# A hybrid decoder step on eight cores: feature-major residual, packed weights, six token tiles, grouped attention and three merged mixer streams

## What is computed

```python
xp = xp + 0.5 * half_ffn(xp, *ffn1)                       # silu(h @ w_gate) * (h @ w_up) @ w_down
qa, ka, va, hq, hf, hi, mq, zg = split_in(rmsnorm(xp, g_mix[l]) @ w_in[l])
for g, (win, dil) in enumerate(((128, 1), (512, 4), (2048, 16))):
    o, s = dilated_group_prompt(qa[:, :, g], ka[:, :, g], va[:, :, g], win, dil)   # 128-query blocks, own and previous block
att = combine_groups(outs, lses)                          # weighted by the softmax denominators
q, k, v, logf = hgrn2_gates(hq, hf, hi, lb)               # f = lb + (1 - lb) * sigmoid(z_f), q = sigmoid(z_q)
o_hg, S = hgrn2_prompt(q, k, v, logf)                     # S_t = diag(f_t) S_{t-1} + k_t v_t^T, chunks of 64
mk, mv = mem_kv(mem_prompt, g_mem[l], w_mem_k[l], w_mem_v[l])
o_mem = mem_attend(mem_heads(mq), mk, mv)                 # 256 memory tokens
xp = xp + merge_branches(att, head_rmsnorm(o_hg, g_hg_out[l]), o_mem, zg, *bw)     # 3 sigmoid gates, then w_out
xp = xp + 0.5 * half_ffn(xp, *ffn2)
```

## Time and profile before

| | us |
|---|---|
| median of 3 timed runs, slowest core | 2612.9 |
| lowest and highest of them | 2612.16, 2627.3 |
| span of the profiled execution, slowest core (core 1) | 2633.5 |
| spans of the other seven cores in it | 2591.5 to 2614.6 |

### The profile page before, as it was taken

One profiled execution on the slowest core, in us unless ns is written; L12 is line 12 of the kernel. 1 busy time (PEld: TensorE's weight loads), 2 busy tenths in 40 slices (PEclk: granted clock), 3 DMA queues, 4 the chain that ended last, 5 costly groups with the idle time before them and its releaser, 6 DMA issues.

```text
span 2633.5 us, 33854 instructions; the slowest of 8 cores (2591.5 to 2633.5 us)
## 1 busy us (share of the span) xinstructions
PE 2112.1 (80%) x11967; PEld 1020.2 (39%) x11967; DVE 806.8 (31%) x1655; ACT 730.6 (28%) x1384; POOL 228.0 (9%) x277
## 2 busy tenths in 40 slices
PE   2799977997299888757696444489999499999995
PEld 2344433442144444432233222334444144444443
DVE  1511111114034445512112445434444322111115
ACT  1511011103033333424216656522220411011104
POOL 1011100110000000110100000021100011111100
PEclk8799988999598998868798666589999699999997
DMA  9366897579334444650753332163325455766543
GB/s 160 73 75 67 81 91 87 65 70 66 37 61 89 89 85 84 95 79 19 125 157 41 128 96 80 40 65 37 37 33 143 86 77 64 75 82 80 58 48 129
DMA packets 312963, 207.56 MB, mean 79 GB/s; under 512 B 179648, under 2 KB 293824, under 8 KB 311264
## 3 DMA queue, kind: packets, MB, share of 16 engines
q0 software_dynamic: 277408, 108.02, 37.4%
q1 hardware_dynamic: 24864, 94.19, 15.0%
q10 hardware_dynamic: 10528, 3.18, 0.9%
HBM read 281.03 MB, written 76.32 MB: 136 GB/s over the span
## 4 chain that ended last, share of the span: by engine, by line
PE 66%; DMA 12%; ACT 7%; DVE 6%; issue 5%; ACTq 2%; another core or an unknown queue 1%; DVEq 0%; POOL 0%; SPq 0%; POOLq 0%
PE ps L559 12%; PE ps L537 11%; PE ps L541 11%; PE ps L587 10%; PE ps L1265 7%; DMA xd_scratch<-xT 4%; PE ps L1268 3%; PE ps L614 3%; PE ps L1295 2%; DMA wp<-w_ff_gate 2%; ACTq L454 1%; PE ps L1155 1%; DMA stg<-x_p 1%; DMA sw1k<-cw1k 1%; ACT L499 1%
## 5 line engine op out<-in xcount | busy, mean ns | idle before, releaser
L541 PE MATMUL ps<-hT,wp 128*128 128x512 bf16 (+1 forms) x1760 | 354.5, 339 | 26.6 <-DMA wp<-w_ff_up 23.2
L537 PE MATMUL ps<-hT,wp 128*128 128x512 bf16 (+1 forms) x1760 | 355.2, 339 | 11.3 <-DMA wp<-w_ff_gate 4.7
L587 PE MATMUL ps<-hT,wp 128*128 128x512 bf16 (+1 forms) x1440 | 275.1, 346 | 62.5 <-ACT xT L710 54.6
L559 PE MATMUL ps<-aarena,wp 128*128 128x512 bf16 (+1 forms) x1760 | 313.4, 336 | 0.0
L547 DVE TENSOR_TENSOR aarena<-ps,f32r 128x512 bf16<-128x512 f32 (+1 forms) x220 | 124.6, 583 | 511.5 <-PE ps L541 510.3
L545 ACT ACTIVATE f32r<-ps 128x512 f32<-128x512 f32 (+1 forms) x220 | 112.7, 512 | 531.2 <-PE ps L537 531.2
L541 PEld LDWEIGHTS ps<-hT,wp 128*128 128x128 bf16 x1760 | 150.5, 98 | 197.8 <-issue 36.1
L537 PEld LDWEIGHTS ps<-hT,wp 128*128 128x128 bf16 x1760 | 150.1, 98 | 180.5 <-issue 19.5
L559 PEld LDWEIGHTS ps<-aarena,wp 128*128 128x128 bf16 x1760 | 146.7, 97 | 166.2
L587 PEld LDWEIGHTS ps<-hT,wp 128*128 128x128 bf16 x1440 | 122.4, 99 | 200.4 <-issue 74.1
L1265 PE MATMUL ps<-hT,wp 128*128 128x512 bf16 (+1 forms) x960 | 192.4, 340 | 5.8 <-ACT f32r L1271 4.8
(11 more groups left out here) (216 smaller groups left out, 2252.5 us busy)
## 6 DMA issues: line engine op xcount, KB each, us to landing
wp<-w_ff_gate POOLq DMA_DIRECT2D x44, 512.0 KB, 8.1
wp<-w_ff_up POOLq DMA_DIRECT2D x44, 512.0 KB, 9.9
wp<-w_ff_down POOLq DMA_DIRECT2D x32, 704.0 KB, 9.1
wp<-w_in POOLq DMA_DIRECT2D x60, 256.0 KB, 6.8
wp<-w_in POOLq DMA_DIRECT2D x10, 1024.0 KB, 12.1
stg<-x_p SPq DMA_DIRECT2D x16, 512.0 KB, 4.0
xd_scratch<-xT SPq DMA_DIRECT2D x4, 2048.0 KB, 35.5
y_p<-stg SPq DMA_DIRECT2D x16, 512.0 KB, 2.6
```

Of the source, the lines that this page charges most:

```text
L537: P.op(PE, lambda e, c=c, gv=gv, pg=pg, t0=t0, n=n: e.matmul(pg.t[:, :n], lhsT=gv[:, c, :], rhs=hT[:, c, t0:t0 + n], start=(c == 0), stop= ...
L541: P.op(PE, lambda e, c=c, uv=uv, pu=pu, t0=t0, n=n: e.matmul(pu.t[:, :n], lhsT=uv[:, c, :], rhs=hT[:, c, t0:t0 + n], start=(c == 0), stop= ...
L559: P.op(PE, lambda e, j=j, dv=dv, pd=pd, off=off, n=n: e.matmul(pd.t[:, :n], lhsT=dv[:, j, :], rhs=act[:, j, off:off + n], start=(j == 0), ...
L587: P.op(PE, lambda e, c=c, pb=pb, t0=t0, n=n: e.matmul(pb.t[:, :n], lhsT=wv[:, c, :], rhs=srcT[:, c, t0:t0 + n], start=(c == 0), stop=(c == ...
```

## The change

The kernel is written anew on the same recording layer.

- **Layout.** Inputs and outputs are packed on the host: `x_in` and `y_out` are feature-major, each of six token tiles (`TOFF`, `TW`: 340 to 344 tokens, the sample tokens in the last) in one stretch per partition, and every weight lies in DRAM as one long row per partition and buffer. All transposes of inputs and outputs are gone from PE, and with them the tile of 4 columns. Two halves of three tiles each take the place of the halves of two and three.
- **Buffers.** PSUM is one pool of 8 banks, weights have 6 buffers of 3072 columns. A pool's slot is taken when the scheduler places the instruction, not when it is recorded.
- **Norms.** Squares go to ACT, DVE or POOL, are added up in float32 on DVE or POOL (`SumSq`) while the down projection still runs, and one matmul per tile sums over partitions.
- **Spill.** The residual is written to DRAM piece by piece (48 pieces of about 342 columns, `down_one`), each after its down projection, and read back per tile (`reload`).
- **Attention.** For 512 queries of one head the numerators of all three groups add up in one PSUM bank, through strided output columns; the probabilities are added on DVE or POOL first, and one matmul with ones gives the denominator. Values are projected token-major with `ht` as the stationary side (`tok_bank`, strided token columns), 2048 matmuls of 128 columns; `tokmajor_pass` and the transposes of v are gone.
- **HGRN.** One head at a time; sigmoids are made of Exp and Ln, so that the mixer uses one table on ACT; the state is cast by ACT or POOL.
- **Streams.** Attention, HGRN and memory are recorded as three streams; `Prog.merge` spreads their priorities over one common stretch, and the scheduler mixes them. Elementwise work can be left to the scheduler to put on ACT, DVE or POOL (`P.flex`).
- **Start and copies.** The loads of x are followed on SP by 20 of the 48 window copies, which wait for no computation; the others are paced.

```diff
-TG = [(0, 512), (512, 512), (1024, 512), (1536, 512), (2048, 4)]
+TOFF = [0, 342, 684, 1024, 1366, 1708]
+TW = [342, 342, 340, 342, 342, 344]
+HALF = [(0, 1, 2), (3, 4, 5)]
+QT = [(0, 416), (416, 416), (832, 416), (1248, 400), (1648, 404)]
...
+    def alias_slots(self, slots, olds):
...
+    def merge(self, windows):
+        tot = sum(self.streams.values())
+        for o in self.all:
+            s = o["stream"]
+            if s is not None:
+                a, b = windows[s]
+                fr = (o["prio"] + o["lead"]) / max(self.streams[s], 1.0)
+                o["prio"] = self.tpe + (a + (b - a) * fr) * tot - o["lead"]
+                o["stream"] = None
...
+                    if st is not None and st != tset[0]:
+                        pen = self.TSW * 4
...
-    wring = Ring([Buf(nc.alloc_sbuf_tensor(f"wp{i}", [128, 4608], BF16), 6) for i in range(3)])
-    f32r = Ring([Buf(nc.alloc_sbuf_tensor(f"f32r{i}", [128, 512], F32)) for i in range(8)])
-    psr = Ring([Buf(nc.alloc_psum_tensor(f"ps{i}", [128, 512], F32), psum=True) for i in range(6)])
+    ps = P.pool("ps", [nc.alloc_psum_tensor(f"ps{i}", [128, 512], F32) for i in range(8)], psum=True)
+    wp = P.pool("w", [nc.alloc_sbuf_tensor(f"wr{i}", [128, 3072], BF16) for i in range(6)])
+    fw = P.pool("fw", [nc.alloc_sbuf_tensor(f"fw{i}", [128, 512], F32) for i in range(8)])
...
+    s4 = P.pool("s4", [xrb(i * 4096, 4096) for i in range(8)] + [xrb(HA * 4 + i * 4096, 4096) for i in range(3)])
+    s1 = P.pool("s1", [xrb(HA * 4 + 12288 + i * 1024, 1024) for i in range(18)])
+    sq4 = P.pool("sq4", [xrb(HA * 4 + 30720 + i * 256, 256) for i in range(8)])
...
-                    P.dma(POOL, lambda e, gv2=gv2, j=j: e.dma_start(out=gv2, in_=wg_v[:, :, j * 128:(j + 2) * 128]), writes=wb.ds)
+    def wload(src, ncols, lead=45000.0):
+        b = wp.new()
+        P.dma(POOL, lambda e: e.dma_start(out=b.t[:, 0:ncols], in_=src), writes=[b.d], lane="w", lead=lead)
+        return b
...
-    def rstd_of(srcT_fn, n, dsrc, nchunks=8, denom=1024.0):
-        pb = ps()
-        for c in range(nchunks):
...
+            q = fw.new()
+            square(lambda: q.t[:, 0:n], lambda: src, [dsrc], [q.d], self.engs)
+            if self.acc is None:
+            tt(lambda: a.t[:, 0:n], lambda: a.t[:, 0:n], lambda: q.t[:, 0:n], ALU.add, [q.d, a.d], [a.d], engs=(DVE, POOL))
...
+        if spill:
+            P.dma(SP, lambda e: e.dma_start(out=xd[ti, :, dp * n:(dp + 1) * n], in_=xc(ti, dp)), reads=[dx[ti][dp]],
+                  writes=[dxd[ti][dp]], lane="spill")
...
-    def load_tokmajor_to_T(src_ap, nrows, dstT, tok0, ddst):
-        sb = stage.next()
-        P.dma(SP, lambda e: e.dma_start(out=sb.t[0:nrows, :], in_=src_ap), writes=[sb.d])
...
+            P.dma(SP, lambda e, q=q: e.dma_start(out=xr[:, ti * XW + q * w * n:ti * XW + (q + 1) * w * n],
+                                                 in_=x_in[ti, :, q * w * n:(q + 1) * w * n]),
+                  writes=dx[ti][q * w:(q + 1) * w], lane="in", lead=200000.0 - ti)
...
-    def tokmajor_pass():
...
+            if g == 2:
+                blocks = [(4 * R + j, 16) for j in range(4)]
+            elif g == 1:
+                blocks = [(512 * R + j, 4) for j in range(4)]
+            else:
+                blocks = [(512 * R + 128 * j, 1) for j in range(4)]
+            pb = tok_bank(wv, blocks, wd)
...
-        pts = {0: scores(0)}
-        for tile in range(16):
-            if tile + 1 < 16:
-                pts[tile + 1] = scores(tile + 1)
-            pv(tile, pts.pop(tile))
+        for r in range(16):
+            mm(lambda r=r: num.t[:, r:512:16], lambda r=r: v16.t[:, r * 128:(r + 1) * 128], lambda r=r: P16.t[:, r * 128 + 32 * R:r * 128 + 32 * R + 32],
+               False, False, [v16.d] + P16.ds, [num.d])
+        for r in range(4):
+            i4 = R * 4 + r
+            mm(lambda r=r: num.t[:, r:512:4], lambda i4=i4: v4.t[:, i4 * 128:(i4 + 1) * 128], lambda r=r: o4.t[:, r * 128:(r + 1) * 128],
+               False, R == 0 and r == 3, [v4.d, o4.d], [num.d])
...
+        den = ps.new()
+        mm(lambda: den.t[:, :], lambda: ones_b[:, :], lambda: ns.t, True, True, [ns.d, dob], [den.d])
+        rc = recip(den, 512)
...
-            P.op(ACT, lambda e, qg=qg, pbq=pbq: e.activation(out=qg.t[:, :n], in_=pbq.t[:, :n], func=AF.Sigmoid), reads=[pbq.d], writes=[qg.d])
...
+        actf(lambda: lq(), lambda: pq.t[:, 0:n], AF.Exp, [pq.d], [lq.d], scale=-1.0)
+        actf(lambda: lq(), lambda: lq(), AF.Ln, [lq.d, dvc], [lq.d], bias=onec)
...
-            nsb = Sbf4_r.next()
-            P.op(ACT, lambda e, nsb=nsb: e.copy(out=nsb.t, in_=S4[:, :]), reads=d_S, writes=[nsb.d])
+                evac(sv, S, [dS[h]], [nb.d], engs=(ACT, POOL))
...
+    P.begin("att")
+    for s in range(4):
+        att_head(s)
+    P.end()
+    P.begin("hg")
+    for h in range(4):
+        hg_head(h)
+    P.end()
+    P.begin("mem")
+    kvs = mem_prep()
+    for h in range(4):
+        mem_head(h, kvs[h])
+    P.end()
+    P.merge({"att": (0.0, 1.0), "hg": (0.03, 0.97), "mem": (0.0, 0.95)})
+
+
...
+    while bulk:
+        s_, d_ = bulk.pop()
+        dd = Dep()
+        P.dma(SP, lambda e, s_=s_, d_=d_: e.dma_start(out=d_, in_=s_), writes=[dd], lane="bulk", lead=400000.0)
```

More of the change, by code:

```diff
@@ L23, in __init__, with new, deps, d @@
         self.psum = psum
-        self.name = name
+        self.vb = vb
+class Slot:
+    def __init__(self, t):
+        self.t = t
+        self.init = set()
+        self.prev = []
+        self.free_at = 0.0
+        self.busy = False
+class Pool:
+    def __init__(self, name, aps, psum=False):
+        self.name = name
+        self.slots = [Slot(a) for a in aps]
+        self.psum = psum
+        self.made = []
+    def new(self, nd=1):
+        v = VBuf(self, nd)
+        self.made.append(v)
+        return v
+    def deps(self):
+        return [d for v in self.made for d in v.ds]
+class VBuf:
+    def __init__(self, pool, nd):
+        self.pool = pool
+        self.t = pool.slots[0].t
+        self.ds = [Dep(pool.psum, self) for _ in range(nd)]
+        self.left = 0
+        self.slot = None
+        self.first = None
+        self.last = {}
+        self.dmas = []
+        self.fin = 0.0
+    @property
+    def d(self):
+        return self.ds[0]
 def _free(ap):
@@ L116, in _add @@
                 for j in d.r:
-                    if self.all[j]["eng"] != eng:
+                    if not (len(engs) == 1 and self.all[j]["engs"] == engs):
                         preds.add(j)
@@ new lines, in slot_for @@
+        def slot_for(v, now):
+            p = v.pool
+            best = None
+            nfree = 0
+            for s in p.slots:
+                if s.busy or (s.init and not all(done[j] for j in s.init)):
+                    continue
+                nfree += 1
+                t = s.free_at
+                if s.init:
+                    t = max(t, max(ops[j]["t1"] + self.SEM for j in s.init))
+                if best is None or t < best[0]:
+                    best = (t, s)
+            if best is None:
+                return None
+            if not any(u is v for u in p.un[:nfree]):
+                return None
+            return best
@@ new lines, in evac, with tt @@
+    def evac(o, i, rd, wr, engs=(ACT, DVE)):
+        alts = {}
+        if ACT in engs:
+            alts[ACT] = lambda e: e.copy(out=o(), in_=i())
+        if DVE in engs:
+            alts[DVE] = lambda e: e.tensor_copy(out=o(), in_=i())
+        if POOL in engs:
+            alts[POOL] = lambda e: e.tensor_copy(out=o(), in_=i())
+        P.flex(alts, reads=rd, writes=wr)
+    def tt(o, a, b, op, rd, wr, engs=(DVE,)):
+        f = lambda e: e.tensor_tensor(out=o(), in0=a(), in1=b(), op=op)
+        P.flex({x: f for x in engs}, reads=rd, writes=wr)
@@ new lines, in stt, with square @@
+    def stt(o, a, s, b, op0, op1, rd, wr):
+        P.op(DVE, lambda e: e.scalar_tensor_tensor(out=o(), in0=a(), scalar=s, in1=b(), op0=op0, op1=op1), reads=rd, writes=wr)
+    def square(o, i, rd, wr, engs=(ACT, DVE)):
+        alts = {}
+        if ACT in engs:
+            alts[ACT] = lambda e: e.activation(out=o(), in_=i(), func=AF.Square)
+        for x in (DVE, POOL):
+            if x in engs:
+                alts[x] = lambda e: e.tensor_tensor(out=o(), in0=i(), in1=i(), op=ALU.mult)
+        P.flex(alts, reads=rd, writes=wr)
@@ new lines, in build_nc @@
+    load_x(0, 4)
+    P.dma(ACT, lambda e: e.dma_start(out=vec[:, :], in_=vec_in[:, :]), writes=[dvec], lane="a", lead=200000.0)
+    load_x(1, 2)
+    load_x(2, 2)
+    for ti in range(3, 6):
+        load_x(ti, 1)
+    norm_first(0, True)
+    norm_first(1, False)
+    norm_first(2, False)
+    P.op(DVE, lambda e: e.tensor_tensor(out=lb, in0=l1, in1=l0, op=ALU.subtract), reads=[dvec], writes=[dvc])
+    P.op(ACT, lambda e: e.activation(out=lb, in_=lb, func=AF.Exp), reads=[dvc], writes=[dvc])
```

2211 lines of the change are left out of this document (1106 added, 1105 removed).

## The result

| | before | after |
|---|---|---|
| median of the timed runs (us) | 2612.5 (2608.6 to 2627.3, 4 runs) | 1911.0 (1910.4 to 1936.6, 4 runs) |
| ratio, with its 95% interval | 1 | 0.7334 (0.7283 to 0.7384) |
| profiled execution, span | 2633.5 | 1909.6 |

The kernel takes 27% less time. 1850 was forecast, with 1720 to 2070 as the range; 1911 is 3.3% above the forecast. Of the 61 us, 49 lie in the span (1910 for the 1861 of the sum), and the windows of the new trace, cut at the same stages as the earlier trace rows, show where; the other 12 are the step from span to time, taken up behind the experiments. Columns: from:to, length, busy us (instructions) of PE, PEld, DVE, ACT, POOL, granted clock, share of the DMA engines, GB/s.

A forecast was written before the change was run, and what follows sets the result against it. PE was taken to bound the kernel, with a floor of 1677 us; start 50, copies 20, spill 15 + 30, mixer stalls 50, tail 15 and joints 4 gave 1861 of span, 1850 as time (range 1720 to 2070).

The forecast's parts named there:

- Tail: End of the kernel: after the last matmuls only a norm and a store remain, 15 us (10 to 25).
- The start: Before PE is dense: 46 us to load x tiles and weights, 4 for the norm's chain, 50 (30 to 80).
- Rival C: Whole kernel: full clock not granted once pauses are gone; 0.85 adds 296 us, so 2140; chance 0.04.
- D: Whole kernel slower than before: weights held at 43 GB/s all through, 2680 us with the start; chance 0.02.
- B: Mixer bound by its dependency chains: PE 60% busy, mixer 763 us, kernel 2100; chance 0.14.
- A: Whole kernel: packed weights, six buffers and three streams hide copies, spill and mismatch; 1732 us; chance 0.24.
- Copies: First feed-forward: 20 window copies (14.7 MB) beside weights leave half the engines, costing 20 us (0 to 40).
- Spill: Residual writes delay what follows: 15 us after the first half (0 to 40), 30 at the mixer's start (0 to 60).
- At the measured rate (63 GB/s for all engines): Down projection: a half's 4.2 MB residual write takes 67 us of engine time beside 47 for weights, within 76 us.
- Mixer: Attention, recurrence and memory: 458 us of PE work, 50 of small stalls (0 to 150), about 540 us long.
- 442 + 7, and 9 more: PE work in the mixer: columns, per-matmul cost, and extra for 644 matmuls of 32 columns or fewer; 458 us.
- POOL: Mixer: some 65 two-input operations on POOL at 1.2 us each; busy 135 us of 540, so no bound.

The follow-up runs named there:

- experiment 5: The changed kernel with the residual spilled as one write per tile (1.4 MB) instead of 24 pieces per half: 1912.3 us, ratio 0.7279.
- experiment 7: The changed kernel with the eight 64-row matmuls of each recurrence tile given one priority, to stand side by side: 1891.3 us, ratio 0.7205.

## Why the prediction was right, and where its terms were off

**Right by its mechanism.** PE sets the time and its work was counted well where it is dense: 456, 304 and 456 us were forecast for the second feed-forward (457 measured), merge and output projection (314, with 45 short matmuls of the mixer, 4 us, in it) and the first feed-forward (474 in the run without the copies, 12 of them the mixer's). Tail and clock held: 13 for 15, 0.975 to 0.980 on all cores, 1.00 in dense windows. The start held as a sum, 46 for 50: tiles 0 to 2 of x had landed at 37 us where 46 were reckoned for all data, and the norm with PE's first matmuls took 9 more where 4 were reckoned. Rival C is out. The limit of 13/16 of which the Trainium skill (TensorE: Matmul & The Clock Gate, Part 1) speaks doesn't show in this execution: from 1440 to 1897 us all eight cores are dense (452 to 456 of 457 us) at 1.00. D is out. B failed by its size: PE is busy for 94% of the mixer, not 60. A is out because of the copies and the mixer's work, though its guess on the spill was the better one.

**Copies: mis-sized, 20 for 42 to 46.** The step was "half the engines are too few by a fifth, until the copies are through". Weights did not get half, but 19.3% against 76.3%, 19 GB/s. The upper bound of 40 was reached by the waits alone; the clock of 0.70 in the 24 us of work between them came on top.

**Spill: the step that failed.** "At the measured rate (63 GB/s for all engines)" carried a property of the old write over to a new one in another layout. 45 us forecast, none measured: no stall between 142 and 562, no hole at 562. Nor is it "spread", as the prediction put it: experiment 5 has it unspread and it is free. The low end, 0, was the truth.

**Mixer: 564 for 538, two errors against each other.** Stalls 36 for 50, hole 0 for 30, PE work 528 for 458. At the prediction's prices the matmuls between 562 and 1126 come to 449 us (9 of the 458 were done earlier). The other 79 us are counted in the trace from each matmul's start to the next, less PE's waits: 22 at the 64-row matmuls, their own delay and that of the one before each (2 in the run of experiment 7); 18 in stretches at the lower clock, 1.2 GHz (31 us in all); 12 at the 2,048 matmuls of 128 columns with `ht` as the stationary side; 8 at the other full ones of 128 columns; 6 in float32; 5 at those of 64 columns or fewer; 8 spread over the rest. Where the tokens of the stationary side lie 16 apart, as in the first of these rows, the matmuls start 62.5 ns apart (3.00 us for 48) where 54.6 were reckoned; runs of the others start 56 ns apart.

```profile
572.12 3.16 PE L685 MATMUL ps<-wr,ht 128*128 128x128 bf16 x48
575.12 0.38 PE L685 MATMUL ps<-xr,wr 128*128 128x256 bf16 x2
```

So the step "442 + 7, and 9 more" priced columns and forgot neighbours, the largest single part of its error (22 of 79): what a matmul costs depends on the one next to it. The clock's part had no term in the sum either.

**Sum.** By stages, from 1861: start -4, first feed-forward +25, mixer +26, merge +10, second feed-forward +1, tail -2, and the 7 for norms and joints, which have no window of their own: 1910, the span. But the +25 is copies +25, spill -15 and 15 besides, of which 9 are the mixer's early matmuls; and the +26 is PE's work +70, stalls -14, no hole -30. So 1911 lies near 1850 in part by luck: errors of +121 and -72 met. The last step of the sum was wrong as well: it took 0.8% off because the profiled execution before stood above its median, but now the span of 1909.6 lies on the median of 1911.0. The 11 us taken off are the rest of the miss.

**POOL.** "1.2 us each ... no bound" was low for its own time (1.3 to 1.6 us) and right that POOL is no bound; it left out that VectorE slows down beside it. Without POOL's elementwise work 16 to 20 us go.

## What to carry to other kernels

With a scheduler like this one, a DMA with no dependency is issued as soon as its queue is idle, whatever its priority: give bulk copies a dependency and one at a time, in a stretch whose queue carries nothing that anybody waits for; a low mean share is no licence for bursts. When a scheduler interleaves streams, look in PE's timeline at the pairs that it makes: matmuls of 64 rows belong side by side. The changed kernel with those two edits and nothing elementwise on POOL runs in 1827 us, ratio 0.6965 (0.6938 to 0.6993) of the kernel before and 4.4% under the change itself.
